# Transposes of x and of the decay columns placed between the last units of the input projection

## What is computed

```python
h = rmsnorm(x, mix_pre_g) * (1.0 + sc1) + sh1
proj = h @ w_in
z, xbc, dt_raw, sc_b, sc_c, sc_h, gates = jnp.split(proj, points, axis=-1)
# ssd_branch
xbc = jax.nn.silu(causal_dwconv(xbc, conv_w, conv_b))     # -> x, B, C
a_cs = jnp.cumsum(adt, axis=-1)
decay = jnp.exp(jnp.where(causal, a_cs[..., :, None] - a_cs[..., None, :], -jnp.inf))
scores = jnp.einsum("bclgn,bcsgn->bcgls", cc, bc)
m = scores[:, :, :, None] * decay
y_diag = jnp.einsum("bcgrls,bcsgrp->bclgrp", m, x)
# short_conv_branch
y_sc = sc_b * causal_dwconv(sc_c * sc_h, sc_conv_w)
```

## Time and profile before

| | |
|---|---|
| median of three runs | 1059.93 us |
| span of the profiled execution, first to last instruction | 1056.5 us |
| what lies between the two | 3.4 us (the profiled execution's full time is not printed; its span plus this is taken for it) |
| PE busy | 1025.1 us, 97% of the span |
| DVE, ACT, POOL busy | 556.2, 634.4, 689.8 us |
| mean granted TensorE clock | 0.997 of full speed |

### The profile page before, as it was taken

How to read it: one execution, slowest core, us unless ns; L and a number is a source line. 1 busy time by engine, 2 the same in 40 slices (tenths; PEclk the granted TensorE clock), 3 DMA queues, 4 the chain that set the end, 5 groups by cost and what they waited for, 6 DMA issues and landing times.

```text
span 1056.5 us, 23232 instructions
## 1 busy us (share of the span) xinstructions
PE 1025.1 (97%) x8537; PEld 966.4 (91%) x8537; DVE 556.2 (53%) x1165; ACT 634.4 (60%) x1133; POOL 689.8 (65%) x306
## 2 busy tenths in 40 slices
PE   7999999999999989999999899999989999999998
PEld 5999999988799979999999799998667699999998
DVE  2577625579874435565522542296566735444400
ACT  4555764477774576666645656744566557666642
POOL 2598899811269855988799287790031075988795
PEclk9999999999999999999999999999999999999999
DMA  9988888655547863777687289865201043665563
GB/s 380 383 306 282 273 307 298 235 191 187 174 146 259 282 236 105 273 235 248 204 279 268 80 283 360 330 239 191 99 21 60 1 140 122 217 193 189 168 217 111
DMA packets 62616, 226.43 MB, mean 214 GB/s; under 512 B 6960, under 2 KB 8272, under 8 KB 61264
## 3 DMA queue, kind: packets, MB, share of 16 engines
q1 hardware_dynamic: 61344, 221.23, 60.5%
q10 hardware_dynamic: 1200, 4.23, 1.4%
HBM read 224.35 MB, written 1.08 MB: 213 GB/s over the span
## 4 chain that ended last, share of the span: by engine, by line
PE 75%; issue 9%; POOL 9%; DVE 3%; ACT 3%; DMA 1%; POOLq 0%; ACTq 0%; DVEq 0%; SPq 0%
PE psL L553 68%; POOL WL L505 8%; PE psO L553 3%; PE psS L553 2%; PE psL L1092 1%; DMA ring<-wts 1%; ACT psL L1685 0%; ACT WH L1155 0%; ACT R L1273 0%; PE psS L1036 0%; ACT L1146 0%; DVE sm L2288 0%; PE psS L1063 0%; PE psS L966 0%; DVE CT L2052 0%
## 5 line engine op out<-in xcount | busy, mean ns | idle before, releaser
L505 POOL TENSOR_TENSOR WL<-ring,WH 128x1024 fp32r<-128x1024 f32 (+1 forms) x282 | 670.4, 2399 | 239.8 <-ACT WH L1155 186.7
L553 PE MATMUL psL<-HR,WH 128*128 128x256 f32 (+1 forms) x3096 | 513.5, 278 | 1.8 <-DVE HR L1796 0.9
L553 PEld LDWEIGHTS psL<-HR,WH 128*128 128x128 f32 (+1 forms) x3096 | 452.6, 187 | 7.5 <-issue 4.8
L553 PE MATMUL psL<-HR,WL 128*128 128x256 f32 x1536 | 396.2, 276 | 0.0
L1155 ACT ACTIVATE WH<-ring 128x1024 fp32r<-128x1024 f32 (+1 forms) x210 | 216.5, 1042 | 107.8 <-PE psL L553 71.9
L553 PEld LDWEIGHTS psL<-HR,WL 128*128 128x128 f32 x1536 | 275.2, 188 | 0.0
L553 PE MATMUL psL<-RR,WH 128*128 128x256 f32 x1356 | 205.2, 277 | 2.4 <-DVE RR L1981 1.2
L553 PEld LDWEIGHTS psL<-RR,WH 128*128 128x128 f32 x1356 | 185.5, 187 | 3.8 <-issue 2.8
L553 PE MATMUL psL<-RR,WL 128*128 128x256 f32 x672 | 145.0, 277 | 0.3 <-POOL WL L505 0.3
L2080 DVE SCALAR_TENSOR_TENSOR CT<-psL,par,CT 128x254 f32<-128x254 f32 (+1 forms) x176 | 80.9, 480 | 107.1 <-ACT CT L1463 102.0
L1454 ACT ACTIVATE WH<-ring 128x1024 fp32r<-128x1024 f32 (+1 forms) x88 | 92.9, 1058 | 71.4 <-PE psL L553 68.0
(11 more groups left out here) (274 smaller groups left out, 1122.8 us busy)
## 6 DMA issues: line engine op xcount, KB each, us to landing
ring<-wts SPq DMA_DIRECT2D x285, 512.0 KB, 4.2
adaring<-ada_w SPq DMA_DIRECT2D x80, 512.0 KB, 4.8
R<-ada_w SPq DMA_DIRECT2D x8, 1024.0 KB, 16.2
ring<-wts SPq DMA_DIRECT2D x16, 384.0 KB, 3.8
R<-cum_dram ACTq DMA_DIRECT2D x8, 512.0 KB, 4.1
R<-wts SPq DMA_DIRECT2D x8, 512.0 KB, 6.4
ring<-wts SPq DMA_DIRECT2D x8, 288.0 KB, 2.8
adaring<-wts SPq DMA_DIRECT2D x4, 512.0 KB, 5.2
```

What stands on the lines that cost most here:

```text
L505: nc.gpsimd.tensor_tensor(WL[:, k, 0:n], ring[:, k, 0:n], WH[:, k, 0:n].bitcast(F32), SUB).then_inc(lo_done, 1)
L553: return nc.tensor.matmul(out, lhsT, rhs, start=start, stop=stop)
```

## The change

PE leaves its loop after unit 57. It first waits for everything that the turns need, and for DVE's read of unit 56 (after which the two scratch banks, which DVE had used for the convolution, are free). Then it makes dt_turn and the first x group, then unit 58, the second x group, unit 59, groups three and four, unit 60, groups five and six, unit 61, groups seven and eight, units 62 and 63, and the scores. ACT copies the groups out between its high parts of the same units. The two CUMB loads stay behind unit 63. DVE, POOL and SP have the same instructions in the same order as before.

```diff
-            linear8("in1", 24, 40, h_hi, h_lo)
-
-            pe.wait_ge(par2_in, 16)
-            pe.wait_ge(dt_ready, 1)
-            out = scratch("dt_turn")
...
+            linear8("in1", 24, 34, h_hi, h_lo)
...
+            pe.wait_ge(par2_in, 16)
+            pe.wait_ge(dt_ready, 1)
+            pe.wait_ge(xbc_ready, 8)
+            u = PLAN.at["in1"][1] + 56
+            pe.wait_ge(lin_free[u % 4], u // 4 + 1)
+            turn_steps()
+            turn_x(0)
+            for m in range(58, 64):
+                unit(PLAN.at["in1"][1] + m, PLAN.q("in1") + m, 1, h_hi, h_lo)
+                if m == 58:
+                    turn_x(1)
+                elif m < 62:
+                    turn_x(2 * (m - 58))
+                    turn_x(2 * (m - 58) + 1)
```

`turn_steps` and `turn_x(i)` hold the dt_turn and x_turn code of before, word for word. On ACT:

```diff
-            units("in1", 48, 16, None)
+            units("in1", 48, 8, None)
...
+            for m in range(56, 64):
+                act.wait_ge(lin_done, PLAN.at["in1"][1] + m + 1)
+                high(fed[0])
+                fed[0] += 1
+                if m == 57:
+                    n = SCRATCH["dt_turn"]
+                    act.wait_ge(s_done, n + 1)
+                    A(CD[:, :, :].rearrange("p a b -> p (a b)"), psS[:, n % 2, 0:128], ACT.Copy).then_inc(s_free[n % 2], 1)
+                    turned_x(0)
+                elif m == 58:
+                    turned_x(1)
+                elif 58 < m < 62:
+                    turned_x(2 * (m - 58))
+                    turned_x(2 * (m - 58) + 1)
```

More of the change, by code:

```diff
@@ L776, in _, with turn_steps, turn_x @@
             last.then_inc(s_done, 1)
-            linear8("in1", 24, 40, h_hi, h_lo)
-            pe.wait_ge(par2_in, 16)
-            pe.wait_ge(dt_ready, 1)
-            out = scratch("dt_turn")
[L782 to L788, removed]
+            linear8("in1", 24, 34, h_hi, h_lo)
+            def turn_steps():
+                out = scratch("dt_turn")
+                for n, row in enumerate((5, 5, 3, 3)):
+                    last = nc.tensor.transpose(out[:, 32 * n:32 * n + 32], dts[:, row, (n % 2) * P:(n % 2 + 1) * P],
+                                               pv("ident", 0, 32)[0:32, :])
+                last.then_inc(s_done, 1)
+            def turn_x(i):
                 t, q = divmod(i, 4)
@@ L1251, in _, with turned_x @@
             units("in1", 40, 8, sc_c_bank)
-            units("in1", 48, 16, None)
-            n = SCRATCH["dt_turn"]
-            act.wait_ge(s_done, n + 1)
-            A(CD[:, :, :].rearrange("p a b -> p (a b)"), psS[:, n % 2, 0:128], ACT.Copy).then_inc(s_free[n % 2], 1)
+            units("in1", 48, 8, None)
+            def turned_x(i):
+                n = SCRATCH["x_turn"] + i
+                t, q = divmod(i, 4)
+                act.wait_ge(s_done, n + 1)
+                A(XTOK[:, t, 512 * q:512 * q + 512], psS[:, n % 2, :], ACT.Copy).then_inc(s_free[n % 2], 1)
+                act.wait_ge(s_free[n % 2], n // 2 + 1)
+                act.sem_inc(xtok_ready, 1)
+            for m in range(56, 64):
[4 more added lines that the diff above has]
+                    n = SCRATCH["dt_turn"]
+                    act.wait_ge(s_done, n + 1)
+                    A(CD[:, :, :].rearrange("p a b -> p (a b)"), psS[:, n % 2, 0:128], ACT.Copy).then_inc(s_free[n % 2], 1)
[5 more added lines that the diff above has]
+                    turned_x(2 * (m - 58) + 1)
             def load_cum(i):
```

## The result

| | before | changed | difference |
|---|---|---|---|
| median of 20 runs of each kernel (the three told above are among those of before) | 1059.11 us | 1063.36 us | ratio 1.0041, 95% interval 1.0029 to 1.0054 |
| span of the profiled execution | 1056.5 us | 1062.1 us | +5.6 us |
| the stage, from the last matmul of unit 57 to the first pair's products | 32.31 us | 34.55 us | +2.24 us |

The change costs 0.41%, 3.1 to 5.7 us, an interval that leaves out no change. The forecast was 1062.7 us, +2.75.

A forecast was written before the change was run, and what follows sets the result against it. PE bounds the kernel, then DVE's chain bounds the scores: 5.1 + 6.3 - 10.05 = +1.35 us, plus 1.4 for the clock, gives +2.75 on 1059.93, so 1062.7 us; range 1060.2 to 1064.2.

The forecast's parts named there:

- The breaks: 36 transposes in five places behind units 57 to 61 cost PE 4.8 us, plus 0.3 us for slower matmuls.
- switches: PE going from a unit's matmuls to transposes and back: 0.12 us per break, five times.
- The slow step of 0.118: Matmuls of units behind a break start 0.118 us apart instead of 0.113; up to 0.65 us, taken as 0.3.
- The forecast's lower end of 3.8 us: Cost of all five breaks at 0.44 us a group with no switches.
- DVE's uncovered chain: DVE's work behind unit 63, formerly hidden, delays the third score group; unit 64 starts 6.3 us behind unit 63's end.
- U': End of unit 63 on PE in the changed kernel, put 5.1 us after the matching point before.
- The clock: PE idle 3.3 us before the third score group likely halves its clock for 3.4 us, costing 1.4 us.
- The sum of the stage, +2.75: +1.35 us from breaks and the later scores, plus 1.4 us for the clock.
- From there on I see nothing that would give it back: After the scores all work hangs on PE's and DVE's progress, so the +2.75 us stays in the whole time.
- 1 (no fall): DVE's chain decides at the scores but PE's clock stays up: +1.35 us, 1061.3 us; chance 0.30.
- Rival 2: Breaks nearly free at 3.8 us by hidden weight loads, DVE's chain, no clock fall: +0.05 us, 1060.0 us; chance 0.07.
- Rival 3: DVE's modulation operation goes ahead of POOL's instead of waiting for it, freeing DVE sooner: -0.45 us, 1059.5 us; chance 0.06.

The follow-up runs named there:

- e3: Changed kernel plus fifteen unused products on PE between the second and third score groups; 1059.85 us, ratio 1.0015 to the kernel before.
- e1: Changed kernel with DVE's modulation vectors moved from ahead of the scores to behind the first pair's differences; 1059.37 us, ratio 1.0005 to the kernel before.
- e2: Kernel before with DVE's modulation vectors moved from ahead of the scores to behind the first pair's differences; ratio 0.9993 to the kernel before.
- e6: Changed kernel with DVE's modulation vectors and last vector-product step behind the first pair's differences, first CUMB load behind unit 61; 1057.90 us, ratio 0.9992 to before.
- e8: e6 with ACT's signal that CD is copied given right behind its copy; 1058.33 us, ratio 0.9999 to the kernel before.
- e12: e8 run again unedited; 1057.35 us, ratio 0.9986 to the kernel before.
- e4: Kernel before with units 58 to 63 as straight code instead of in the loop, turns still behind them; 1059.5 us, ratio 1.0001 to before.

## Why the prediction was right, and where it was off

The sign, the mechanism and the range held, but the closeness of the number is in part luck. The forecast started from 1059.93 us, while the 20 runs of before have a median of 1059.11: the change is +4.25 us, not +2.75, and the stated range laid over 1059.11 would end at 1063.4, just above the 1063.36 measured. The 3.4 us put between span and time were too much as well: in nearly all runs with both on record the time is 1.7 to 1.9 us over the span. And three of the terms missed in ways that partly cancel. Step by step:

- **The breaks, 4.8 + 0.3 us: measured 4.4.** Their places were right, and so was that no copy holds PE up. This is the step that was mis-sized, in the x groups and in the switches. Inside a group the transposes start 0.109 us apart, so a group costs 0.44 us, the lower end of the forecast's own span, and the eight 3.5 us for 3.85. The switches were 5 x 0.12 = 0.6 us in the forecast and are about 0.25 on the chip. Into dt_turn there is 0.20 us (192.86 to 193.06), 0.09 over an ordinary step, and the first step of the x group behind it takes 0.16, 0.05 over; into an x group there is nothing (207.04 to 207.16 is 0.12). Coming back there is next to nothing: the unit's first matmul starts 0.03 us behind the last transpose and its second 0.20 us later, 0.23 us together, as long as two ordinary steps. The other breaks add some hundredths each. The slow step of 0.118 shows in three of the six units (60, 62 and 63), 0.3 us, as taken. The forecast's lower end of 3.8 us is 3.9 by its own terms (0.36 + 8 x 0.44). The Trainium skill, page "TensorE: Matmul & The Clock Gate", section "Step-by-step: what each phase is for", was set against the trace in the prediction and there set aside. For the way into an x group and the way back its rule of weight loads pulled ahead holds; for the way into the 32-row turns and the 64-column products, 0.21 us each, the trace shows more than a step.
- **DVE's uncovered chain: right.** DVE was to read the first group 4.15 us behind U' and PE to start the third at U' + 4.9; with U' = 213.69 it was 4.34 and 5.08. Unit 64 was to start at U' + 6.3; without the fall it does so at U' + 6.5 (e3), with it at U' + 6.8. e1 and e2 show that it is this chain, and that it was free before.
- **The clock: right that it falls, its price somewhat low.** The forecast took 1.4 us, with ends of 1.1 and 1.7. The short fall costs 1.6 to 1.7, the long one, for which no row of before spoke, 2.5 to 2.75; the mean is 2.0. The chance given, somewhat over a half, was modest for what came five times in five.
- **The sum of the stage, +2.75: 2.24 in the profile shown, 2.66 in the mean of five.** The mean comes near because the breaks' 0.7 us too much and the clock's 0.6 too little offset each other; unit 64 comes 0.2 us later than forecast and the first pair 0.2 us sooner behind it (both in e3, which has no fall).
- **"From there on I see nothing that would give it back": nor does anything, but more is lost than the stage shows.** Mean against mean it is +3.8 us, and 1.1 us of it lie outside the stage (1.6 by the ratio). The means of e1, e3, e6, e8 and e12 are also 1 to 2.4 us over what their stages say, those of e2 and e4, which leave the turns where they were, 0.4 and 0.6. Each of these numbers is uncertain by 1 to 1.7 us, so it is only all together that they suggest that the extra time goes with the moved turns and not with the pause. Part of it is clock: the 59 runs of kernels with moved turns and no fall at the stage have a mean granted clock of 0.9958 for 0.9964 before, which is an estimated 0.7 us lost at other places. Where the rest lies, and why, is open: the last matmul of unit 57 starts between 192.6 and 195.3 us, and from the first pair's products to the last instruction a single execution takes 831.2 or 831.6 us in the kernel before and 829.9 to 834.7 in the changed one, more scatter than what is sought.

Of the rivals, 1 (no fall) was not seen once; without the fall the change costs 0.64 us at the stage (e3), under its 1.35 because the breaks were cheaper and the steps of unit 64 and the next shorter. Rival 2's rule held for all ways but that into dt_turn, yet the breaks cost 4.4 us, not its 3.8, and the clock fell. Rival 3's mechanism, an operation of DVE that lasts as long as POOL's, is shown by 1.93 against 0.18 us, but the order of the two did not turn. The Trainium skill, page "SBUF — State Buffer", section "Who interferes with whom", says that of DVE and GpSimd whichever began first keeps the shared pair for its whole instruction, and the trace agrees: L1924 ends 0.05 us behind POOL's operation, which began first.

## What to carry to other kernels

Before work is moved out from in front of a wait, look at which other engine did something in that time: what was hidden behind the removed work is the new critical path, and it should be moved, or made early, in the same edit (e6 and e8 did, and turned +2.2 us of stage into -2.7, though the whole time gained at most 1 us of it). Price the idle PE time that is left twice, once as waiting and once for the clock that it costs the work behind it. And where a change is worth 0.2%, believe neither one stage of one profile nor one median: here the whole time of the kernels with moved turns was some 1 to 2 us over what one stage said.

## What the runs showed of the hardware

- A fall of the clock to 0.50 lasts 3.4 us or 6.8 us with one and the same pause of 3.61 us (three and two of five executions); the short ones begin 1.05 to 1.5 us behind its end, the long ones 0.9 and 1.5 us ahead of it. A fall between 761 and 776 us is in all 14 profiles, 3.4 us long in nine and 6.8 in five, and those near 390 and 585 us come in four each. Fifteen idle products in the pause (30 records of 128 columns) kept the clock at 1.00.
- In the shown stretch of before, 6.7 us of transposes and short pauses kept 1.00; so did the 36 transposes between units in every kernel with moved turns.
- The step of the same fp32r matmul is 0.113 or 0.118 us over whole stretches without a wait. It differs from unit to unit in the changed kernel and between kernels that are alike there (unit 64 and the next took 5.83 or 5.63 us). No row names the cause.
- Two groups of four 128x128 transposes run through in 0.79 us, 0.109 from start to start, with nothing lost at the border between two scratch banks; the turns of before took 0.73 us a group because each waited for a copy.
- A vector operation of 32 columns took 1.93 us while a POOL operation that had begun 0.46 us earlier ran, and 0.18 us with POOL idle (e1).
